# Second block's layer norms per token tile: last down half ordered by tile, scale and shift on transposed values, next product in token halves

## What is computed

```python
def layer_norm(x, g, b):
    mu = jnp.mean(xf, axis=-1, keepdims=True)
    var = jnp.mean(jnp.square(xf - mu), axis=-1, keepdims=True)
    y = (xf - mu) * lax.rsqrt(var + LN_EPS)
    return y * g + b
...
    for l in range(DEPTH):                       # DEPTH = 2
        x = layer_norm(ALPHA * x + 0.5 * swiglu(x, ffn1...[l]), ln_g[l, 0], ln_b[l, 0])
        proj = x @ w_in[l]
        u, gb, gc, h, q, k, v = jnp.split(proj, splits, axis=-1)
        y = jnp.concatenate([pool_mixer(u, ...), gated_conv_mixer(gb, gc, h, ...),
                             neighbourhood_attention(q, k, v, rpb[l])], axis=-1) @ w_out[l]
        x = layer_norm(ALPHA * x + y, ln_g[l, 1], ln_b[l, 1])
        x = layer_norm(ALPHA * x + 0.5 * swiglu(x, ffn2...[l]), ln_g[l, 2], ln_b[l, 2])
```

## Time and profile before

| | |
|---|---|
| median of 3 runs (lowest to highest) | 3396.62 us (3394.16 to 3401.14) |
| profiled execution, its own time | 3401.0 us |
| its span, first to last instruction | 3399.2 us |
| PE busy / DVE busy / ACT busy / POOL busy | 90% / 42% / 28% / 4% |
| mean granted TensorE clock | 0.952 |
| chain that ended last, by engine | PE 80%, DVE 13%, ACT 3%, issue 2%, POOL 1%, DMA 1% |

### The profile page before, as it was taken

One profiled execution on the slowest core, in us unless ns is written; L12 is line 12 of the kernel. 1 busy time (PEld: TensorE's weight loads), 2 busy tenths in 40 slices (PEclk: granted clock), 3 DMA queues, 4 the chain that ended last, 5 costly groups with the idle time before them and its releaser, 6 DMA issues.

```text
span 3399.2 us, 32476 instructions
## 1 busy us (share of the span) xinstructions
PE 3070.6 (90%) x13984; PEld 2475.9 (73%) x13984; DVE 1436.7 (42%) x1904; ACT 948.5 (28%) x1131; POOL 145.4 (4%) x108
## 2 busy tenths in 40 slices
PE   6898998589898979999889799997999979979997
PEld 5777777577686757888765688886888766668885
DVE  4434237733622574233535633335323354543234
ACT  3221323232223222222323322222222233332121
POOL 0010000100100000000300000001000030000000
PEclk9998999799999989999898899998999989989998
DMA  5121111212121203222320122222222241122221
GB/s 189 53 90 62 62 62 50 81 72 86 51 87 38 87 13 118 99 99 99 85 81 22 66 96 99 94 93 96 92 98 99 99 76 50 63 75 99 99 92 69
DMA packets 40574, 275.73 MB, mean 81 GB/s; under 512 B 5428, under 2 KB 5618, under 8 KB 8688
## 3 DMA queue, kind: packets, MB, share of 16 engines
q1 hardware_dynamic: 34560, 251.67, 21.1%
q0 software_dynamic: 5056, 18.32, 2.3%
q10 hardware_dynamic: 816, 3.67, 0.3%
HBM read 269.45 MB, written 2.10 MB: 80 GB/s over the span
## 4 chain that ended last, share of the span: by engine, by line
PE 80%; DVE 13%; ACT 3%; issue 2%; POOL 1%; DMA 1%; ACTq 0%; DVEq 0%; POOLq 0%
PE G L331 14%; PE G L332 13%; PE G L333 13%; PE G L343 10%; PE G L344 10%; PE G L345 10%; PE A L648 1%; DVE w_lo L1038 1%; PE A L669 1%; PE A L476 1%; DVE x L1469 1%; POOL qkv L1657 1%; PE A L379 1%; ACT w_hi L738 1%; DVE x L1466 1%
## 5 line engine op out<-in xcount | busy, mean ns | idle before, releaser
L1038 DVE TENSOR_TENSOR w_lo<-raw,w_hi 128x2048 fp32r<-128x2048 f32 (+1 forms) x240 | 542.8, 2262 | 1115.6 <-ACT w_hi L738 1115.4
L331 PE MATMUL G<-xT_hi,w_hi 128*128 128x512 f32 (+1 forms) x2144 | 844.1, 394 | 31.6 <-ACT work L949 18.0
L332 PE MATMUL G<-xT_lo,w_hi 128*128 128x512 f32 (+1 forms) x2144 | 834.9, 389 | 0.0
L333 PE MATMUL G<-xT_hi,w_lo 128*128 128x512 f32 (+1 forms) x2144 | 834.6, 389 | 0.0
L738 ACT ACTIVATE w_hi<-raw 128x2048 fp32r<-128x2048 f32 (+1 forms) x240 | 451.5, 1883 | 1186.5 <-PE G L345 647.5
L331 PEld LDWEIGHTS G<-xT_hi,w_hi 128*128 128x128 f32 x2144 | 407.8, 190 | 146.5 <-issue 50.5
L333 PEld LDWEIGHTS G<-xT_hi,w_lo 128*128 128x128 f32 x2144 | 407.9, 190 | 82.6
L332 PEld LDWEIGHTS G<-xT_lo,w_hi 128*128 128x128 f32 x2144 | 408.2, 190 | 78.7
L343 PE MATMUL G<-w_hi,h_hi 128*128 128x512 f32 x704 | 278.1, 395 | 0.0
L344 PE MATMUL G<-w_lo,h_hi 128*128 128x512 f32 x704 | 278.1, 395 | 0.0
L345 PE MATMUL G<-w_hi,h_lo 128*128 128x512 f32 x704 | 278.0, 395 | 0.0
(11 more groups left out here) (258 smaller groups left out, 3224.4 us busy)
## 6 DMA issues: line engine op xcount, KB each, us to landing
raw<-in_stream SPq DMA_DIRECT2D x240, 1024.0 KB, 4.8
lnr<-in_ln_rows POOLq DMA_DIRECT2D x6, 1024.0 KB, 5.7
row<-in_rows POOLq DMA_DIRECT2D x6, 512.0 KB, 7.9
fA<-in_mem POOLq DMA_DIRECT2D x2, 1024.0 KB, 7.5
x<-in_x ACTq DMA_DIRECT2D x1, 2048.0 KB, 10.7
out<-x POOLq DMA_DIRECT2D x1, 2048.0 KB, 7.1
qkv<-work POOLq DMA_DIRECT2D x32, 62.0 KB, 7.5
cst<-in_const ACTq DMA_DIRECT2D x1, 1474.0 KB, 13.8
```

The lines of the kernel that those rows point to most:

```text
L331: mm(o, a, hi[:, c, 0:n], start=start, stop=False)
L332: mm(o, a, lo[:, c, 0:n], start=False, stop=False)
L333: return mm(o, wl[:, col:col + P], hi[:, c, 0:n], start=False, stop=stop)
L1038: tt(w_lo[:, s, 0:nk, :], raw[:, s, 0:nk, :], w_hi[:, s, 0:nk, :].bitcast(F32), ALU.subtract).then_inc(lo_done, 1)
```

## The change

1. **Order by tile.** The last half of each second down product is walked in `FF_ORDER` and the second half of the output product in `OUT_ORDER`, so that banks 0 and 1 are done earlier. Each tile is measured, normed and transposed for itself; the transposes of tiles 0 and 1 stand inside this half.
2. **Scale and shift after the transpose.** PE transposes z. There gain and shift are one number per partition, and ACT applies them while it reads PSUM (`normed_operand`: two activations of 128x256 and a copy of 128x512 for each of four banks, twice). x itself gets them later, by DVE alone (`residual`), behind units of the next product. POOL does no norm work any more.
3. **Token halves.** The unit behind the norm is done for tokens 0 to 255 and then 256 to 511 (`gemm_token_halves`), all its products with 256 columns; the transposes of tiles 2 and 3 stand inside it. Both its weight blocks stay in use until the second token half.
4. **Bias earlier.** The eight bias products stand ahead of and inside the last down half; `shifted` has its own place (over `y2_lo`), is cleared early, and its transfers are issued as soon as ACT has copied the rows.
5. **Output.** SP writes each tile out as it is ready, in place of one transfer by POOL.

```diff
@@ PE @@
+            def turn_normed(L, t):
+                pair, i = divmod(t, 2)
+                pe.wait_ge(S["ln_z"], 4 * L + t + 1)
+                for c in range(DCH):
...
+                    last = nc.tensor.transpose(A[:, c // 2, (c % 2) * 256 + i * P:(c % 2) * 256 + i * P + P],
+                                               x[:, t, c * P:c * P + P], I)
...
+            def gemm_token_halves(L, jobs):
...
+                for p in range(2):
+                    for b in range(2):
+                        s = (Pos.off + b) % 2
+                        if p == 0:
+                            pe.wait_ge(lo_done, 2 * Pos.pair + Pos.off + b + 3)
+                        pe.wait_ge(S["v_lo"], 8 * L + 4 * p + 2 * b + 2)
+                        for n, (bank, emits) in enumerate(jobs[p]):
...
+                            if p and n == len(jobs[p]) - 1:
+                                last.then_inc(blk_used, 1)
...
+                            if p == 0 and b and n == 1:
+                                turn_normed(L, 2)
+                                turn_normed(L, 3)
...
+            FF_ORDER = ((0, 0), (0, 1), (0, 2), (0, 3), (1, 0), (2, 0), (1, 1), (2, 1), (1, 2), (1, 3), (2, 2), (2, 3))
+            OUT_ORDER = ((0, 0), (0, 1), (1, 0), (1, 1), (0, 2), (0, 3), (1, 2), (1, 3))
...
+                        def between(i):
+                            if L % 3 == 0 and i == 1:
+                                bias(1)
+                            if L < 3 * DEPTH - 1 and i in (8, 9):
...
+                                turn_normed(L, i - 8)
+                        gemm_last_half(downs, FF_ORDER, h_hi, h_lo, between)
@@ ACT @@
+            def normed(L, t):
+                rsqrt(1, t, preload=False)
+                act.wait_ge(S["ln_bias"], 4 * L + t + 1)
+                fn(x[:, t, :], x[:, t, :], ACT.Identity, scale=rs_r[:, t:t + 1],
+                   bias=nmx[:, 0, t:t + 1]).then_inc(S["ln_z"], 1)
+            def layer_norm(L):
+                normed(L, 0)
+                normed(L, 1)
+                if L < 3 * DEPTH - 1:
+                    split()
+                    normed_operand(L, 0)
+                    split()
+                normed(L, 2)
+                normed(L, 3)
...
+                    normed_operand(L, 1)
@@ DVE @@
+            def residual(L, t):
...
+                dve.wait_ge(S["ln_z"], 4 * L + t + 1)
+                link(tt(x[:, t, :], x[:, t, :], lnr[:, 0, :], ALU.mult))
+                tt(x[:, t, :], x[:, t, :], lnr[:, 1, :], ALU.add).then_inc(S["x_res"], 1)
+            def layer_norm(L, scale, eps):
+                for t in (0, 1):
+                    measured(t, scale, eps)
+                    scaled(t)
+                if L < 3 * DEPTH - 1:
+                    split()
+                    low_parts(L, 0, (0, 1))
+                    measured(2, scale, eps)
+                    low_parts(L, 0, (2, 3))
+                    scaled(2)
+                    measured(3, scale, eps)
+                    scaled(3)
+                    split()
+                    low_parts(L, 1, range(4))
...
+                for n in range(3):
                     unit(none, K2)
+                    for t in ((0,), (1,), (2, 3))[n]:
+                        residual(3 * l, t)
@@ ACT @@
+                act.wait_ge(S["x_res"], 4 * (3 * l + 1))
```

More of the change, by code:

```diff
@@ L181, in build @@
         nmx = sb("nmx", [P, 4, 32], on=two)
+        lnc = sb("lnc", [P, 3 * DEPTH, 2, 8], on=two)
         with ExitStack() as over:
@@ new lines, in scaled, with low_parts @@
+            def scaled(t):
+                newton(1, t)
+                stt(out=nmx[:, 0, t:t + 1], in0=mean_var[:, t, 0:1], scalar=-1.0, in1=rs_r[:, t:t + 1],
+                    op0=ALU.mult, op1=ALU.mult).then_inc(S["ln_bias"], 1)
+            def low_parts(L, pair, banks):
+                for bank in banks:
+                    dve.wait_ge(S["v_hi"], 8 * L + 4 * pair + bank + 1)
+                    part = slice(2 * bank, 2 * bank + 2), slice(256 * pair, 256 * pair + 256)
+                    tt(xT_lo[:, part[0], part[1]], xT_f[:, part[0], part[1]],
+                       xT_hi[:, part[0], part[1]].bitcast(F32), ALU.subtract).then_inc(S["v_lo"], 1)
```

363 lines of the change are left out of this document (222 added, 141 removed).

## The result

The changed kernel takes 3339.25 us (median of 4 runs, 3335.94 to 3343.26); beside it the kernel before took 3398.3 us, a ratio of 0.984 with a 95% interval of 0.982 to 0.985. Run again later, it took 3335.78 us against 3398.56, 0.981 (0.979 to 0.984). So it is faster by 57 to 63 us (the 57 against the median of 3396.62 us that stands ahead of the prediction) where 81 were forecast. The direction is right, but the forecast of 3315 us is 24 too low, and the time lies 14 us above the upper end of the forecast's range (3304 to 3325).

A forecast was written before the change was run, and what follows sets the result against it. TensorE (90% busy) was taken to bound the kernel, standing mostly idle for 24.40 to 25.63 us at each of five norms and waiting for bias transfers. Savings of 101.4 less 15 and 5 gave 81.4: 3396.62 becomes 3315.2 us, range 3304 to 3325.

The forecast's parts named there:

- a bank of ScalarE's operand: In the split unit behind each norm: one bank of normed_operand takes ScalarE 1.25 us, four take 5.
- a layer's bias products: At norms 0 and 3: the bias products add 1.8 us to the time around the norm.
- one wait a unit ended by `w_lo`: Inside every split unit: TensorE waits once, 3 to 5 us, for the low part of the second weight block.
- the bias transfers hidden: Ahead of the q unit: earlier issue removes the 18.0 us wait in two layers; 19.0 us saved with clock and lateness counted.
- Rival B: Ahead of the q unit: bias transfers still end the wait, the 19 us come back, 3334 us; chance 0.06.
- Rival C: In all five split units: TensorE stays at 1.2 GHz, making the kernel slower, 3418 us; chance 0.03.
- Rival D: Over the whole kernel: no low clock and half of the pooling delay hidden, 3303 us; chance 0.12.
- Low clock: Behind the new waits of 2 to 4 us: the clock may fall, 5 us lost in all, bounds 0 and 10.
- rival A: In ScalarE's operand banks: small steps are dear, a bank takes 1.9 us, 15 us lost in all, 3330; chance 0.17.
- Pooling: Behind the v unit: scaling x delays the first scores, 7.5 us with low clock, 15 lost in two layers.
- q's second block: In the q unit: building bm stands ahead of this block's split, making it 1.4 us late in each layer.
- several small waits that it overlooked: No place named: small waits missed by the forecast bring the time to 3335 to 3380 us; chance 0.07.

The follow-up runs named there:

- experiment 4: Changed kernel with GpSimd issuing the 16 bias transfers only once tile 3 is normalised, about as late as before the change: 3367.93 us against 3339.25.
- experiment 6: Changed kernel with the last down half by blocks again and tiles 0 and 1 turned behind its last product: 3367.43 us against 3339.25.
- experiment 5: Changed kernel with the unit behind each norm done in whole after all four tiles are turned, not in token halves: 3371.4 us against 3339.25.
- experiment 3: Changed kernel with all x tiles of a layer's first norm scaled behind the q and k units, none behind v: 3321.48 us against 3339.25; again, 3322.38.
- experiment 2: Changed kernel with one plain copy per bank on ScalarE, gain and shift of the operand left out of the computation: 3335.49 us against 3339.25.
- experiment 8: Changed kernel with lnc (384 bytes a partition) placed behind y2_lo, so h and y2 regain their old addresses: 3344.32 us against 3339.25.
- Experiment 1: Changed kernel with the split unit's second block split earlier, between banks 1 and 2 on ScalarE, ahead of banks 2 and 3 on VectorE: 3324.62 us against 3339.25.
- experiment 9: Changed kernel with the edits of experiments 1, 3, 7 and 8 together: 3283.43 us, ratio 0.968 to the kernel before.
- experiment 7: Changed kernel with VectorE splitting q's second block in the middle of building bm, not behind it: 3338.07 us against 3339.25.

## Where the prediction was right, and why it was too low

**The step that failed** is the pricing of what stands between the last half and the end of the split unit, not the path: the sum takes 1.25 us for a bank of ScalarE's operand, which took 1.57, and 1.8 us for a layer's bias products, which took 3.9. These two terms are some 11 of the 17 us that the stages fall short; the rest is spread over smaller ones.

**Right.** The forecast saw the change as it is: no wait at the half's end at norms 1 and 4, one wait a unit ended by `w_lo` (3.4 us where 3 to 5 were written), the scores late by 8.4 us in each layer (6 to 8 written, so a little outside), the end 9.4 us sooner (8.4), and the bias transfers hidden, which experiment 4 prices at 19.7 us against 19.0. Two of its signs of being wrong came true as well: steps of 128x256 at 0.5 us or more (0.55), and waits for `xT_lo` in the second token half of norms 1, 2 and 4 (0.7 us each). Rival B (transfers still end the wait) is out by that. Rival C (slower, at 1.2 GHz) is out: the clock over the five stretches is 0.95 to 1.00. The granted clock does fall behind most of the 3.4 us waits, for some 18 products at a time. The Trainium skill (TensorE: Matmul & The Clock Gate, section "A second HAM failure mode: psum-queue depth-cycling") tells of swings between the two levels when TensorE idles shortly between groups of products; that the clock swings, the traces agree. Rival D is out, since the pooling delay wasn't hidden at all. The order by tile is worth 23 us and the token halves 26 by the stages of experiments 6 and 5; neither could be read from the diff alone.

**Too low by these terms of the sum.** The stages that the program sets came to 64.2 us (the table without the first block and the neighbourhood's stretches), 17.2 less than 81.4:

- *Low clock, 1.4.* I took 5. Slow products are there for 10.0 us: 3.4 each at norms 0 and 3, 1.6 each at 1 and 4, nothing at 2. But 3.6 of that, behind the wait that stands ahead of the unit at norms 0 and 3, delay nothing. Norm 3 shows it, first in after, where these products are slow, then in the second trace of experiment 3, whose instructions in this unit are the same and where they run at full clock:

```profile
2685.85 0.36 PE L354 MATMUL G<-w_hi,xT_hi 128*128 128x256 f32 x1 [2.29 <-issue]
...
2696.70 0.45 PE L354 MATMUL G<-w_hi,xT_hi 128*128 128x256 f32 x1 [3.10 <-DVE w_lo L1190]
```

```profile
2677.49 0.35 PE L354 MATMUL G<-w_hi,xT_hi 128*128 128x256 f32 x1 [2.29 <-issue]
...
2683.55 0.39 PE L342 MATMUL G<-xT_hi,w_hi 128*128 128x256 f32 x1 [1.52 <-DVE x L1568]
...
2688.35 0.38 PE L354 MATMUL G<-w_hi,xT_hi 128*128 128x256 f32 x1 [3.10 <-DVE w_lo L1190]
```

  From the unit's first product to the end of the wait for `w_lo` it is 10.85 and 10.86 us: at full clock TensorE waits 1.8 us for bank 3 instead. What the clock cost is 6.4.
- *Bias products, 4.2.* The sum had 1.8 us for eight products. Each product is two instructions, and the trace of after has them as two groups of eight ahead of and within the half:

```profile
1628.73 1.94 PE L725 MATMUL A<-poolw,work 15*128 15x248 f32 x8
...
1636.40 1.94 PE L725 MATMUL A<-poolw,work 15*128 15x248 f32 x8
```

  That is 3.9 us a layer more in the half. The trace of before has two groups of eight as well, and only one was counted.
- *ScalarE's bank, some 7.2.* The step of 128x256 with scale and bias takes 0.55 us (0.45 from one to the next) and not 0.38 and 0.30, the copy behind it 0.63; a bank comes each 1.57 us and not each 1.25. At norm 2 `w_lo` of the second block came at T = 43.2 and not at 42.0, and the low parts of tiles 2 and 3 left a wait of 0.7 where the sum had 0.05; at norms 1 and 4 it is 1.3 each. At norms 0 and 3 it is some 1.4 each: 0.3 at the wait ahead of the unit, 0.6 at the waits for bank 3 and `w_lo` (4.9 as they are without the slow products, 4.35 in the sum) and 0.5 at that for the second token half. This is rival A at half of its size, as the bank is halfway between 1.25 and 1.9. Experiment 2 shows that this step sets a good part of these waits: with a bank each 1.15 us they were 0.3 us shorter ahead of norm 2's unit (2.36 from product to product, not 2.69) and 0.8 ahead of norm 0's second token half (1.43, not 2.27). The trace of before had no such step. The Trainium skill (ScalarE: Activation LUTs, section "What ACT_TABLE_LOAD costs") gives 186 ns, 93 more for each per-partition operand and 0.833 ns a column, with 93 ns of overlap. Estimated from these figures the step takes 0.585 us, 0.49 from one to the next, and the bank 1.5. The trace, 0.55 and 1.57, is near. The price halved from a 512-column row was too low: in the rows of experiment 2 a plain step of 512 columns takes 0.58 us, and one of 256 with scale and bias 0.55.
- *The address of the held operand, 2.6*, which nothing in the diff's text or in the trace of before could show (experiment 8).
- *Pooling, 1.9.* 8.45 us a layer and not 7.5: the two tiles took 4.9 us as forecast, and the products behind the wait ran at half the clock.
- *q's second block, 1.4.* It was late by 2.1 in each layer (2.3 from product to product) and not by 1.4.
- The end was better by 1.0. Together that is 17.7 where 17.2 are missing; the 0.5 between them has no cause that I could name.

**Beside the sum.** The profiled run of before was 4.4 us above its median (3396.62), that of after 3.1 below; so these medians differ by 57.4 and not by 64.8. In these 64.8 the neighbourhood's stretches, which the forecast had at nothing, gave 5.6 and the first block took 5.0, and neither is the change's doing as far as the other traces show. A second pair of medians differs by 62.8.

**Overlooked, without cost.** PE also waits for bank 3 (up to 1.5 us), because VectorE adds tile 3 only behind the Newton step of tile 2. The longer wait for `w_lo` took it in. Experiment 1 moved that add as well; the earlier split without it was not run. The prediction put the outcome of several small waits that it overlooked at 3335 to 3380 us with a chance of 0.07; the time fell there, by terms it had named and priced too low for the most part.

## What to carry to other kernels

When a wait is cut into pieces, price what remains of each piece with the clock behind it, and ask for each engine in turn what stands ahead of the instruction that ends it: here one split and one pair of scalings, moved into time that the engines had, were worth 36 us by their stages (32 by the medians), more than half of what the whole change brought. Slow products cost nothing where the engine would have waited behind them anyway, so the clock's price is read to the end of the next wait. An edit of a few microseconds is judged by its own stage in the trace, between fixed points; the total can move by 10 us through stretches that it never touches. An operation that no trace shows is priced by its fixed part and its part by columns, not by halving a longer one.

## What the runs showed of the hardware

**The clock behind a wait.** In eleven traces, every wait of PE in or ahead of a split unit, by its length from product to product, and how often a slow stretch followed before the next wait. A slow stretch is 15 to 27 products of 256 columns that start 0.21 us apart where 0.12 is full clock; behind each of the other waits there were at most three such starts.

| wait, us | times | with a slow stretch |
|---|---|---|
| 0.7 to 1.8 | 64 | 0 |
| 2.3 to 2.4 | 25 | 8 |
| 2.6 to 2.7 | 28 | 13 |
| 3.3 to 3.4 | 42 | 36 |
| 4.2 to 4.9 | 3 | 3 |

No slow stretch followed a wait below 2 us; between 2.3 and 3.4 us the same wait was followed by none at one place and by 1.3 to 1.9 us of slow products at another (up to 2.6 in experiment 6). In a second trace of the changed kernel the same six places were slow again (the first twelve products' pitch at norms 0, 0, 1, 3, 3, 4: 0.152, 0.202, 0.185, 0.168, 0.217, 0.215 us in the one, 0.153, 0.202, 0.186, 0.166, 0.215, 0.184 in the other) and all others were not, so it isn't chance alone; what decides it stays open. The two levels are the 2.4 and 1.2 GHz of the granted clock.

**A stretch that no edit touched.** The 400 products from the first scores to the output product, same instructions and same order in every kernel. The second trace of the kernel before (layer 0, layer 1), then experiment 1 (layer 0), then experiment 9 (layer 1):

```profile
1789.46:1892.44 102.98, 95.44 (x400) 58.96 (x400) 56.77 (x166) 38.56 (x104) 0.00 (x0) 0.87 0.05 18
2850.06:2943.25 93.19, 85.63 (x400) 53.75 (x401) 56.59 (x166) 38.66 (x104) 0.00 (x0) 0.96 0.05 20
```

```profile
1778.09:1881.41 103.32, 96.12 (x401) 59.45 (x401) 56.87 (x166) 38.62 (x104) 0.00 (x0) 0.85 0.03 11
```

```profile
2763.27:2856.19 92.92, 85.35 (x400) 53.59 (x400) 56.60 (x166) 38.68 (x104) 0.00 (x0) 0.96 0.05 19
```

VectorE's and ScalarE's busy times are the same to 0.3 us; the length goes with the granted clock, 93 us at 0.96 and 103 at 0.85 to 0.87. Over fourteen traces both layers together took 192 to 205 us. That spread alone is more than experiments 7 and 8 were worth. What sets the clock there from one kernel to the next stays open.

**The address of the still operand.** Products that hold h or y and move 512 weight columns start 0.2333 us apart with the held operand at its old address (four traces) and 0.2343 with it 384 bytes further (ten traces), at full clock. Why is open; other distances weren't tried.
